# Shift rows laid down first and added by the gather, router products in column tiles, last turns between dense tiles

## The chip, the cores and the metric

The kernel runs on one core of a Trainium2 chip. The metric is the device time of one execution in microseconds (us), the median of three runs. Times inside the kernel come from one profiled execution. PE is TensorE, DVE is VectorE, ACT is ScalarE, POOL is GpSimd; SP only issues transfers. 2.4 GHz and 1.2 GHz are the two levels of TensorE's clock, shown as granted clock 1.00 and 0.50.

## The reference

One layer of a diffusion backbone with 128 context tokens and 512 latent tokens of width 2048: attention and gMLP side by side, an output projection, then a mixture of 16 experts in which each expert chooses its tokens. Everything is fp32. What the change touches:

```python
h2 = rms(x, p['g_ffn']) * (1 + sc2) + sh2
aff = softmax(h2 @ w_router)                   # 16 experts
gate, idx = top_k(swapaxes(aff, 1, 2), cap)    # 64 latent + 16 context rows for each expert
xg = h2[idx]
y = (silu(xg @ w_e1) * (xg @ w_e3)) @ w_e2 * gate
x = x + gate2 * scatter_add(y, idx)            # then a final rms and the outputs
```

`sc2` and `sh2` (scale and shift) are one row each for the context tokens and one for the latents.

## The kernel before, in words

Four phases follow one another, with a barrier at the end of each: front (adaLN rows and input projection), heads (attention), projects (three dense products, the last of which is the output projection) and experts. fp32 weights come in pieces of 128x2048 (1.05 MB). ScalarE makes a rounded high part of each (`w_hi`), VectorE the low part (`w_lo`), and PE multiplies three times (high with high, high with low, low with high; lines 107 to 109, the function `product`).

**Projects (`phase_projects`).** Chunks of 512 output columns, four pieces for each chunk, five row tiles (`t`, the first is context) for each piece. In the last dense product (`OUT`) the new residual rows are stored by POOL from `side` into `xn` in HBM, multiplied with the gain (`gained`, VectorE, into `M.xg`), turned by PE (`turn_xg`, four transposes of 128x128), copied by ScalarE (`xg_turned`), and multiplied with the router's weights (`route`: four products of 128 rows, 16 columns, accumulated in PSUM, output 16x128). VectorE adds the result of a chunk into `M.logitT` (`logit_added`). For the first three chunks these steps lie between the dense tiles of the third piece of the next chunk; for the last one all five turns and routes follow behind the last dense tile. POOL waits for the stores of `xn` before the barrier.

**Experts (`phase_experts`), its start.** PE turns `M.logitT` back into rows; VectorE scales them by 1/rms, adds the shift's logits, finds softmax and then the picks (eight rounds over the latents and two over the context, line 2132 on). ScalarE scales the rows `h_row` by 1/rms (`scale_rows`, three buffers for five tiles), POOL adds the shift row to each (line 1892) and stores it to `h` in HBM (line 1894). When all are stored and the picks are there, POOL gathers the first expert's 80 rows into `xg` (line 1876). SP has meanwhile begun to load weight pieces into eight slots; slot and order are fixed, piece n is issued when piece n-8 is split (line 91).

**Experts, the loop.** For expert i the body has 24 pieces (j = 0 to 23): eight for `w_e1` of the next expert, eight for `w_e3` of the next expert, eight for `w_e2` of this one. ScalarE and VectorE work three pieces ahead of PE in three buffers. Behind piece 16 PE turns the first twelve sixteenths of the rows of expert i+2 (`turn_rows`, line 2235), behind piece 20 the rest; that frees `xg`. VectorE makes the output rows `expert_y` at j = 19 and 23 (`out`, line 2082) from the products, `gate_now` and `gate2`. POOL's queue in iteration i is: gather of expert i+2; copies of the row numbers and gates of expert i (lines 1881, 1882, the semaphore `idx_s`, which `out` awaits); the scatter of expert i with addition into `xn` (line 1885); the wait until it has landed.

**Experts, the tail.** The last expert's rows are not scattered: POOL gathers the rows of `xn` that they belong to (line 1913), loads `xn` tile by tile (`f_x`, line 1907), ScalarE and VectorE normalise these and POOL stores the outputs; last come the rows of the last expert.

The tiles `c_st` (the front's stationary columns, 128x16x32) and `ident` stay in SBUF through all phases. The front already has products in column tiles (line 736): four products whose outputs are partitions 32j to 32j+31.

Of the kernel before, what the change touches and what calls it, by code (L numbers as in the profile page):

```python
# [14 lines left out]
P = 128  # L15
# [1281 lines left out]
def phase_projects(nc, M, I, W):  # L1297
# [8 lines left out]
    w_r = m.new("w_router_sb", [P, KT, EXPERTS], F32)  # L1306
# [5 lines left out]
    M.logitT = m.new("logitT", [EXPERTS, N_TOK], F32)  # L1312
# [18 lines left out]
    with ExitStack() as ctx:  # L1331
# [7 lines left out]
        gate_in, stored = M.pool_sem("proj_gate_in"), [M.pool_sem(f"proj_stored{t}") for t in range(TT)]  # L1339
        turn_out = [M.pool_sem(f"proj_turn_out{b}") for b in range(2)]  # L1340
# [26 lines left out]
        @block.sync  # L1367
        def _(sp):
            def load_w(n):
                if n >= 4:  # L1370
                    sp.wait_ge(w_split, n - 3)
                sp.dma_start(stage(n), WT[n // PER][(n % PER) // KG, n % KG]).then_inc(w_in[n % 4], 16)

            def load_x(s, g):
                if x_at(s, g) >= 2:
                    sp.wait_ge(x_l, x_at(s, g) - 1)
                if s == MLA and g == 0:
                    for b in range(2):
                        sp.wait_ge(M.o_out[b], 16 * (HEADS // 2))
                if s == OUT:  # L1380
                    for b in range(2):
                        sp.wait_ge(turn_out[b], 16 * ((TT * (g + 1) + 1 - b) // 2))
                src = XT[s].rearrange("(g j p) n -> g p j n", g=KG, j=KG)[g]
                sp.dma_start(x_raw[:, g % 2], src).then_inc(x_in[g % 2], 16)

            for g in range(KG):
                load_w(g)
                load_x(GM, g)
            for n in range(KG, N_PIECES):
                load_w(n)  # L1390
                s, r = n // PER, n % PER
                if s == MLA and r == KG:
                    sp.dma_start(w_r[:], I["w_router"][0].rearrange("(k p) n -> p k n", p=P)).then_inc(w_r_in, 16)
# [12 lines left out]

        @block.gpsimd
        def _(pool):
# [51 lines left out]
            for t in range(TT):  # L1460
                pool.wait_ge(stored[t], 16 * 2 * N_CH)
# [84 lines left out]
        def _(dve):  # L1546
# [40 lines left out]
            def logit_added(i):  # L1587
                dve.wait_ge(logit, TT * i + TT)
                if i:
                    dve.wait_ge(logit_sum, 2 * i)  # L1590
                for a, b, src in ((0, P, ps[6][0:EXPERTS, 0:P]), (P, N_TOK, ps[7][0:EXPERTS, :])):
# [72 lines left out]
        def _(pe):  # L1664
# [67 lines left out]
            for n in range(N_PIECES):  # L1732
# [3 lines left out]
                for t in range(TT):  # L1736
# [22 lines left out]
def phase_experts(nc, M, I, W, O):  # L1759
# [5 lines left out]
    h_row = [m.new(f"h_row{b}", [P, D], F32) for b in range(3)]  # L1765
    shift = m.new("shift2_rows", [P, 2, D], F32)
# [43 lines left out]
    with ExitStack() as ctx:  # L1810
# [7 lines left out]
        sum2, var, std, inv, scaled = (sem(f"r_{n}") for n in ("sum2", "var", "std", "inv", "scaled"))  # L1818
        log_tr, log_ok, top, neg, ex, ex_inv, aff_ok, aff_tr, aff_ev, picked, picks, pick_tr, pick_ok = (
            sem(f"r_{n}") for n in ("log_tr", "log_ok", "top", "neg", "ex", "ex_inv", "aff_ok", "aff_tr", "aff_ev", "picked", "picks", "pick_tr", "pick_ok"))  # L1820
        shift_in, h_ok, h_out = sem("r_shift_in"), sem("r_h_ok"), [M.pool_sem(f"r_h_out{b}") for b in range(3)]
# [10 lines left out]
        def _(sp):  # L1832
# [13 lines left out]
            for r in range(2):  # L1846
                sp.dma_start(shift[:, r, :], M.mod[r:r + 1, 3 * D:4 * D].to_broadcast((P, D))).then_inc(shift_in, 16)
            for q in range(PB):
                load(q, q, E13[0][0, q])
# [18 lines left out]
        def _(pool):  # L1868
            pool.sem_inc(y_free, 1)
            pool.sem_inc(x_tr, 3)  # L1870

            def gather(e):
                pool_wait(pool, x_tr, 3 * e + 3, passed)
                pool.tensor_copy(cur_g[:], rows[:, bass.ds(e, 1)]).then_inc(idx_g, 1)
                pool_wait(pool, idx_g, e + 1, passed)
                pool.indirect_dma_start(out=xg[:], out_offset=None, in_=M.h2,
# [18 lines left out]
            for b in range(3):  # L1895
                pool.wait_ge(h_out[b], 32 if b < 2 else 16)
# [11 lines left out]

            pool.tensor_copy(cur_s[:], rows[:, LAST:LAST + 1]).then_inc(idx_s, 1)
# [5 lines left out]
            for t in range(N_F):  # L1915
# [23 lines left out]
        def _(act):  # L1939
# [35 lines left out]
            def scale_rows(t):  # L1975
                if t >= 3:
                    act.wait_ge(h_out[t % 3], 16)
                for i in range(4):
                    act.activation(h_row[t % 3][:, bass.ts(i, NC)].rearrange("p (j n) -> p j n", j=KG), M.xg[i][t], ACT.Copy,  # L1979
# [70 lines left out]
        def _(dve):  # L2050
# [60 lines left out]
            dve.wait_ge(log_tr, 1)  # L2111
            for t in range(TT):
                dve.scalar_tensor_tensor(logits[:, t, :], pair[1][:, 0, bass.ts(t, EXPERTS)], st[:, 3, t:t + 1], M.shift_logit[:, min(t, 1), :],
# [108 lines left out]
        def _(pe):  # L2222
# [63 lines left out]
            for t in range(TT):  # L2286
                ins = pe.transpose(pair[1][:, 0, bass.ts(t, EXPERTS)], M.logitT[:, bass.ts(t, P)], M.ident[0:EXPERTS, 0:EXPERTS])
# [191 lines left out]
```

## Time and profile before

| | |
|---|---|
| median of 3 runs | 3500.28 us (3500.27 to 3500.41) |
| profiled execution | 3501.81 us, span 3500.0 us |
| PE busy | 3288.2 us (94%) |
| VectorE busy | 2108.0 us (60%) |
| ScalarE busy | 1409.6 us (40%) |
| POOL busy | 363.6 us (10%) |
| transfers | 790 MB, mean 226 GB/s |

The span is what the profile covers; 1.8 us of the execution lie around it, and the profiled execution is 1.5 us above the median. A busy PE is not PE at its peak: ends of matmuls are modelled, so their durations overlap, and I read the cost of a step from the start of one instruction to the start of the next. "Landing" is the time from a transfer's issue until all of it has arrived. "DMA share" is the mean busy share of the 16 DMA engines; it can read a little above 1.

### The profile page before, as it was taken

The numbers are of one execution on the slowest core, as the hardware profiler recorded it, in microseconds if no ns is written. First come the engines' busy times: TensorE is split into PE (matmuls) and PEld (weight loads), VectorE is DVE, ScalarE is ACT, GpSimd is POOL, SyncE is SP. The second block draws the span as 40 slices with busy tenths as digits, with TensorE's granted clock in tenths as the row PEclk, the third lists the DMA queues.
The fourth block names the chain that finished last, engine by engine and source line by source line (L and its number), as shares of the span: only waits on it lengthen the run. The fifth ranks groups of instructions, "written<-read, shape, count | busy, mean of one in ns | idle before, by whom it ended". The sixth has DMA issues, their size and how long they took to land. (4 is left out here: it accounts for less than half of the span.)

```text
span 3500.0 us, 39964 instructions
## 1 busy us (share of the span) xinstructions
PE 3288.2 (94%) x16088; PEld 2556.1 (73%) x16088; DVE 2108.0 (60%) x1830; ACT 1409.6 (40%) x1295; POOL 363.6 (10%) x429
## 2 busy tenths in 40 slices
PE   6889999999998899998999999939999999999995
PEld 4678878888886899986888888725666666666663
DVE  3336555555553677753232243257888898888886
ACT  3122212221211444442121222236777777777774
POOL 0020010010100000000011111030112111111102
PEclk9999999999999999999999999969999999999997
DMA  9465545465542111106253444168999999999996
GB/s 381 182 167 200 189 172 189 150 237 191 199 171 104 69 37 42 36 22 259 102 193 132 145 167 146 58 254 320 375 396 382 386 400 383 385 399 395 385 405 225
DMA packets 142462, 790.13 MB, mean 226 GB/s; under 512 B 18992, under 2 KB 30288, under 8 KB 61408
## 3 DMA queue, kind: packets, MB, share of 16 engines
q1 hardware_dynamic: 101680, 668.72, 49.5%
q0 software_dynamic: 40656, 119.60, 11.2%
q8 instruction: 95, 1.56, 0.2%
q14 instruction: 31, 0.25, 0.0%
HBM read 720.39 MB, written 67.86 MB: 225 GB/s over the span
## 5 line engine op out<-in xcount | busy, mean ns | idle before, releaser
L102 DVE TENSOR_TENSOR w_lo<-w_stage,w_hi 128x2048 fp32r<-128x2048 f32 x384 | 880.2, 2296 | 140.5 <-ACT w_hi L97 140.5
L97 ACT ACTIVATE w_hi<-w_stage 128x2048 fp32r<-128x2048 f32 x384 | 736.8, 1920 | 306.2 <-PE e_ps L109 306.1
L107 PE MATMUL i_ps<-w_hi,hT_hi 128*128 128x512 f32 (+1 forms) x1440 | 568.2, 395 | 26.0 <-DVE hT_lo L563 13.5
L108 PE MATMUL i_ps<-w_lo,hT_hi 128*128 128x512 f32 (+1 forms) x1440 | 558.7, 388 | 0.0
L109 PE MATMUL i_ps<-w_hi,hT_lo 128*128 128x512 f32 (+1 forms) x1440 | 558.5, 388 | 0.0
L107 PE MATMUL e_ps<-w_hi,xgT_hi 128*80 128x512 f32 x1024 | 404.0, 395 | 2.5 <-DVE xgT_lo L2052 2.3
L108 PE MATMUL e_ps<-w_lo,xgT_hi 128*80 128x512 f32 x1024 | 403.8, 394 | 0.0
L109 PE MATMUL e_ps<-w_hi,xgT_lo 128*80 128x512 f32 x1024 | 401.2, 392 | 0.0
L107 PE MATMUL p_ps<-w_hi,xT_hi 128*128 128x512 f32 x960 | 379.3, 395 | 15.5 <-DVE xT_lo L1547 15.5
L109 PE MATMUL p_ps<-w_hi,xT_lo 128*128 128x512 f32 x960 | 375.4, 391 | 0.0
L108 PE MATMUL p_ps<-w_lo,xT_hi 128*128 128x512 f32 x960 | 375.3, 391 | 0.0
L568 DVE TENSOR_TENSOR w_lo<-w_raw,w_hi 128x2048 fp32r<-128x2048 f32 (+1 forms) x72 | 161.8, 2247 | 348.7 <-ACT w_hi L439 348.7
L1547 DVE TENSOR_TENSOR w_lo<-w_stage,w_hi 128x2048 fp32r<-128x2048 f32 x48 | 110.0, 2292 | 392.5 <-ACT w_hi L1471 392.5
L439 ACT ACTIVATE w_hi<-w_raw 128x2048 fp32r<-128x2048 f32 (+1 forms) x72 | 135.3, 1879 | 515.1 <-PE i_ps L109 504.6
L107 PEld LDWEIGHTS i_ps<-w_hi,hT_hi 128*128 128x128 f32 x1440 | 273.0, 190 | 87.5 <-issue 26.2
L109 PEld LDWEIGHTS i_ps<-w_hi,hT_lo 128*128 128x128 f32 x1440 | 272.8, 189 | 54.9
L108 PEld LDWEIGHTS i_ps<-w_lo,hT_hi 128*128 128x128 f32 x1440 | 273.4, 190 | 52.5
L580 DVE SCALAR_TENSOR_TENSOR w_stage<-w_stage,csil 128x2048 f32<-128x2048 f32 x120 | 276.4, 2346 | 0.0
L1471 ACT ACTIVATE w_hi<-w_stage 128x2048 fp32r<-128x2048 f32 x48 | 91.9, 1915 | 442.5 <-PE p_ps L109 436.6
L107 PEld LDWEIGHTS p_ps<-w_hi,xT_hi 128*128 128x128 f32 x960 | 181.1, 189 | 52.7 <-issue 16.5
L107 PEld LDWEIGHTS e_ps<-w_hi,xgT_hi 128*80 128x80 f32 x1024 | 152.2, 149 | 86.9 <-issue 2.3
L109 PEld LDWEIGHTS e_ps<-w_hi,xgT_lo 128*80 128x80 f32 x1024 | 152.3, 149 | 84.1 <-issue 1.1
(322 smaller groups left out, 4443.7 us busy)
## 6 DMA issues: line engine op xcount, KB each, us to landing
w_stage<-in_w_e SPq DMA_DIRECT2D x384, 1024.0 KB, 9.3
w_stage<-in_w_ada SPq DMA_DIRECT2D x96, 1024.0 KB, 6.1
w_raw<-in_w_in SPq DMA_DIRECT2D x64, 1024.0 KB, 4.9
w_stage<-in_w_o_gm SPq DMA_DIRECT2D x16, 1024.0 KB, 7.8
w_stage<-in_w_o_mla SPq DMA_DIRECT2D x16, 1024.0 KB, 5.4
w_stage<-in_w_out SPq DMA_DIRECT2D x16, 1024.0 KB, 4.8
acts<-evacuated POOLq DMA_DIRECT2D x60, 256.0 KB, 3.9
side<-acts POOLq DMA_DIRECT2D x40, 256.0 KB, 5.7
```

The costliest lines, as they stand in the source:

```text
L97: act.activation(dst, src, ACT.Copy).then_inc(st.hi, 1)
L102: dve.tensor_tensor(dst, src, hi.bitcast(F32), ALU.subtract).then_inc(st.split, 1)
L107: pe.matmul(out, x_hi, w_hi, start=first, stop=False)
L108: pe.matmul(out, x_hi, w_lo, start=False, stop=False)
L109: return pe.matmul(out, x_lo, w_hi, start=False, stop=last)
L439: act.activation(w_piece(W.hi, n), draw[n % 2][:, 0:KG * WIDTH[n // KG]], ACT.Copy).then_inc(d_hi, 1)
L568: dve.tensor_tensor(w_piece(W.lo, n), draw[n % 2][:, 0:w], w_piece(W.hi, n).bitcast(F32), ALU.subtract).then_inc(d_split, 1)
L580: ins = dve.scalar_tensor_tensor(acc[r], W.stage[:, n % 2, :], csil[:, r, t:t + 1], acc[r], ALU.mult, ALU.add)
L1471: act.activation(W.hi[:, n % 2, :], stage(n), ACT.Copy).then_inc(w_h, 1)
L1547: sub = lambda out, src, hi: dve.tensor_tensor(out, src, hi.bitcast(F32), ALU.subtract)
```

## The change

1. **The shift.** POOL no longer adds the shift to `h_row`; the rows stored to `h` are without it, and SP's two loads of the shift rows are gone. A new step on POOL, `fill`, writes the shift row into all 80 places of `xg` (two transfers with a broadcast source, 64 and 16 rows), and the gather adds to them. The gather waits for its fill (semaphore `filled`). `fill(e)` waits until PE has turned the rows of expert e-1; in the loop it stands between the gather of expert i+2 and the copies and scatter of expert i. `h_row` has five buffers instead of three, so ScalarE's scaling waits for no store.
2. **The router.** Its weights lie in `c_st`, 32 columns for each 128 rows (16 of them used). The four products of `route` go to four column tiles, each a product of its own, instead of being accumulated; `logitT` has 128 partitions, its turn back is five full transposes, and VectorE adds the four groups with two reductions before the scaling.
3. **The last turns.** The turns of the last chunk's first two row tiles, and the route of the first, come between the dense tiles of the last piece (the third turn and second route right behind the last tile).
4. **Waits for the stores of `xn`** move from the end of projects into experts: SP waits ahead of its eighth load, POOL behind its stores to `h`.
5. **Tail.** `load_x(0)` stands ahead of the copies and the gather of the last rows.

```diff
-    w_r = m.new("w_router_sb", [P, KT, EXPERTS], F32)
+    w_r = M.c_st
-    M.logitT = m.new("logitT", [EXPERTS, N_TOK], F32)
+    M.logitT = m.new("logitT", [P, N_TOK], F32)
...
-            for t in range(TT):
-                pool.wait_ge(stored[t], 16 * 2 * N_CH)
...
-                out = ps[7][0:EXPERTS, bass.ts(t - 1, P)] if t else ps[6][0:EXPERTS, 0:P]
+                out = ps[7][:, bass.ts(t - 1, P)] if t else ps[6][:, 0:P]
                 for j in range(KG):
-                    ins = pe.matmul(out, w_r[:, KG * i + j, :], x[:, j, :], start=(j == 0), stop=(j == KG - 1))
+                    ins = pe.matmul(out[32 * j:32 * j + 32, :], w_r[:, KG * i + j, :], x[:, j, :], start=True, stop=True, skip_group_check=True)
...
+                    if n == N_PIECES - 1 and t >= 2:
+                        turn_xg(N_CH - 1, t - 2)
+                        if t >= 3:
+                            route(N_CH - 1, t - 3)
...
-            for t in range(TT):
+            for t in (3, 4):
                 turn_xg(N_CH - 1, t)
-                if t:
-                    route(N_CH - 1, t - 1)
+                route(N_CH - 1, t - 1)
...
-    h_row = [m.new(f"h_row{b}", [P, D], F32) for b in range(3)]
-    shift = m.new("shift2_rows", [P, 2, D], F32)
+    h_row = [m.new(f"h_row{t}", [P, D], F32) for t in range(TT)]
...
+            def fill(e):
+                pool_wait(pool, x_tr, 3 * e + 3, passed)
+                for a, b, r in ((0, CAP_LAT, 1), (CAP_LAT, SLOTS, 0)):
+                    pool.dma_start(xg[a:b, :], M.mod[r:r + 1, 3 * D:4 * D].to_broadcast((b - a, D))).then_inc(filled, 16)
             def gather(e):
-                pool_wait(pool, x_tr, 3 * e + 3, passed)
                 pool.tensor_copy(cur_g[:], rows[:, bass.ds(e, 1)]).then_inc(idx_g, 1)
                 pool_wait(pool, idx_g, e + 1, passed)
-                pool.indirect_dma_start(out=xg[:], out_offset=None, in_=M.h2,
+                pool_wait(pool, filled, 32 * e + 32, passed)
+                pool.indirect_dma_start(out=xg[:], out_offset=None, in_=M.h2, compute_op=ALU.add,
...
-            pool.wait_ge(shift_in, 32)
             for t in range(TT):
                 pool.wait_ge(scaled, 4 * t + 4)
-                pool.tensor_tensor(h_row[t % 3][:], h_row[t % 3][:], shift[:, min(t, 1), :], ALU.add).then_inc(h_ok, 1)
-                pool.wait_ge(h_ok, t + 1)
-                pool.dma_start(M.h2[bass.ts(t, P), :], h_row[t % 3][:]).then_inc(h_out[t % 3], 16)
+                pool.dma_start(M.h2[bass.ts(t, P), :], h_row[t][:]).then_inc(h_out, 16)
...
+            fill(0)
             pool.wait_ge(pick_ok, 2)
             gather(0)
+            fill(1)
             gather(1)
-            with pool.Fori(0, EXPERTS - 2) as i:
+            fill(2)
+            with pool.Fori(0, EXPERTS - 3) as i:
                 gather(i + 2)
+                fill(i + 3)
                 scatter(i)
+            gather(EXPERTS - 1)
+            scatter(EXPERTS - 3)
             scatter(LAST - 1)
...
+            load_x(0)
             pool.tensor_copy(cur_s[:], rows[:, LAST:LAST + 1]).then_inc(idx_s, 1)
...
-            for t in range(N_F):
+            for t in range(1, N_F):
                 load_x(t)
...
-                if t >= 3:
-                    act.wait_ge(h_out[t % 3], 16)
...
+            by_group = lambda ap, n: ap[:, 0:n * P].rearrange("p (t j e) -> p t e j", t=n, j=KG)[:, :, 0:EXPERTS, :]
+            dve.tensor_reduce(logits[:, 0:4, :], by_group(pair[1][:, 0, :], 4), AX.X, ALU.add).then_inc(log_sum, 1)
+            dve.tensor_reduce(logits[:, 4:5, :], by_group(pair[1][:, 1, :], 1), AX.X, ALU.add).then_inc(log_sum, 1)
+            dve.wait_ge(log_sum, 2)
```

## Rows read from the trace of the kernel before

**Rows 1.** Stretches: length; busy PE, PEld, DVE, ACT, POOL; PEclk, DMA share, GB/s.
```profile
2298.00:2353.00 55.00, 3.08 (x16) 1.61 (x17) 35.15 (x82) 22.42 (x36) 26.58 (x12) 0.51 0.94 367
...
2570.00:2638.00 68.00, 68.00 (x314) 44.41 (x313) 60.19 (x32) 48.85 (x30) 10.20 (x5) 1.00 1.01 390
```

**Rows 2.** Chain of waits ahead of the first expert: start us, us, what.
```profile
2334.74 7.71 DMA h<-h_row
...
2343.72 8.89 DMA xg<-h,rows_gather
```

**Rows 3.** Timeline of ScalarE and VectorE there: start us, us, engine, line, operation.
```profile
2310.03 0.70 ACT L1979 ACTIVATE h_row<-xg_last,r_stats 128x512 f32<-128x512 f32 x1
...
2329.72 0.17 DVE L2143 CAST rows<-e_ps 80x16 uint32<-80x16 f32 x1 [0.43 <-PE e_ps L2296]
```

**Rows 4.** Timeline of PE, one route and turn between dense tiles.
```profile
2257.06 1.05 PE L1722 MATMUL p_ps<-more,w_router_sb 128*16 128x128 f32 x8
2258.03 0.66 PE L1710 MATMUL p_ps<-ident,xg_third 128*128 128x128 f32 x4
2258.45 0.48 PE L107 MATMUL p_ps<-w_hi,xT_hi 128*128 128x512 f32 x1
```

**Rows 5.** Timeline of PE in the front: products in column tiles, then a transpose.
```profile
102.79 1.07 PE L736 MATMUL i_ps<-w_stage,c_st 128*32 128x256 f32 x16
103.80 0.44 PE L745 MATMUL i_ps<-ident,mod_rows 128*128 128x128 f32 x2
```

**Rows 6.** Ends of the phases projects and front: timelines, and DRAIN (ns, start us).
```profile
2288.24 0.54 POOL L1442 DMA_DIRECT2D xn<-side  x1 [2.18 <-DVE side L1610]
...
2294.27 0.87 DVE L1593 TENSOR_TENSOR logitT<-logitT,p_ps 16x128 f32<-16x128 f32 x2 [5.52 <-PE p_ps L1722]
...
L1331 POOLq DRAIN  x1: 5850/5850/5850, 2292.6 to 2292.6; - x1
...
1123.12 0.54 POOL L336 DMA_DIRECT2D acts<-evacuated  x1 [2.18 <-ACT evacuated L457]
...
L223 POOLq DRAIN  x1: 6295/6295/6295, 1126.5 to 1126.5; - x1
```

**Rows 7.** DMA view of 2570 to 2638, 40 slices of 1.7 us.
```profile
GB/s 429 424 429 434 414 366 251 246 328 424 424 424 419 419 414 424 424 424 424 424 419 424 419 429 414 419 424 424 414 395 434 414 299 395 366 275 275 251 328 410
DMA packets 3653, 26.51 MB, mean 390 GB/s; under 512 B 417, under 2 KB 417, under 8 KB 417
```

**Rows 8.** DMA view, issues at 2773.7, 2977.4, 2821.7: count, KB, median us to landing.
```profile
w_stage<-in_w_e SPq DMA_DIRECT2D x1, 1024.0 KB, 13.2
...
w_stage<-in_w_e SPq DMA_DIRECT2D x1, 1024.0 KB, 11.8
...
w_stage<-in_w_e SPq DMA_DIRECT2D x2, 1024.0 KB, 7.2
```

**Rows 9.** ScalarE's waits from 2436 to 3381 (us, times, longest), and one instruction.
```profile
ACT w_hi L97 <- PE e_ps L109: 266.1, 335, 1.4
...
2608.14 1.92 ACT L97 ACTIVATE w_hi<-w_stage 128x2048 fp32r<-128x2048 f32 x1 [0.86 <-PE e_ps L109]
```

**Rows 10.** Timeline of VectorE, PE and POOL in one iteration.
```profile
2609.53 1.27 DVE L2082 SCALAR_TENSOR_TENSOR expert_y<-e_ps,gate_now,gate 80x1024 f32<-80x1024 f32 x1
2610.72 2.27 DVE L102 TENSOR_TENSOR w_lo<-w_stage,w_hi 128x2048 fp32r<-128x2048 f32 x1
...
2607.94 0.44 PE L2235 MATMUL e_ps<-ident,xg 80*128 80x80 f32 x4
...
2573.23 2.68 POOL L1876 DMA_INDIRECT xg<-h,rows_gather  x1 [0.81 <-POOL rows_gather L1874]
```

**Rows 11.** Timeline of POOL and ScalarE in the tail.
```profile
3428.46 0.18 POOL L1909 COPY rows_scatter<-rows 80x1 uint32<-80x1 uint32 x1 [9.63 <-DMA xn<-expert_y,rows_scatter]
...
3432.03 3.30 POOL L1907 DMA_DIRECT2D f_x<-xn  x6
...
3442.95 1.03 ACT L2013 ACTIVATE e_ps<-f_x 128x1024 f32<-128x1024 f32 x1 [5.75 <-DMA f_x<-xn]
```

More of the change, by code:

```diff
@@ L1339, in phase_projects @@
         gate_in, stored = M.pool_sem("proj_gate_in"), [M.pool_sem(f"proj_stored{t}") for t in range(TT)]
+        M.xn_stored = stored
         turn_out = [M.pool_sem(f"proj_turn_out{b}") for b in range(2)]
@@ L1392, in _ @@
                 if s == MLA and r == KG:
-                    sp.dma_start(w_r[:], I["w_router"][0].rearrange("(k p) n -> p k n", p=P)).then_inc(w_r_in, 16)
+                    sp.dma_start(w_r[:, :, 0:EXPERTS], I["w_router"][0].rearrange("(k p) n -> p k n", p=P)).then_inc(w_r_in, 16)
                     for h in range(2):
@@ L1590, in logit_added @@
                     dve.wait_ge(logit_sum, 2 * i)
-                for a, b, src in ((0, P, ps[6][0:EXPERTS, 0:P]), (P, N_TOK, ps[7][0:EXPERTS, :])):
+                for a, b, src in ((0, P, ps[6][:, 0:P]), (P, N_TOK, ps[7][:])):
                     if i:
@@ L1817, in phase_experts @@
             sem(f"e_{n}") for n in ("x_tr", "x_hi", "x_lo", "sil_ok", "hid_ok", "h_tr", "h_hi", "h_lo", "y_ev"))
-        sum2, var, std, inv, scaled = (sem(f"r_{n}") for n in ("sum2", "var", "std", "inv", "scaled"))
+        sum2, var, std, inv, scaled, log_sum = (sem(f"r_{n}") for n in ("sum2", "var", "std", "inv", "scaled", "log_sum"))
         log_tr, log_ok, top, neg, ex, ex_inv, aff_ok, aff_tr, aff_ev, picked, picks, pick_tr, pick_ok = (
             sem(f"r_{n}") for n in ("log_tr", "log_ok", "top", "neg", "ex", "ex_inv", "aff_ok", "aff_tr", "aff_ev", "picked", "picks", "pick_tr", "pick_ok"))
-        shift_in, h_ok, h_out = sem("r_shift_in"), sem("r_h_ok"), [M.pool_sem(f"r_h_out{b}") for b in range(3)]
+        filled = M.pool_sem("rows_filled")
+        h_out = M.pool_sem("r_h_out")
         f_in, f_out, g_in = [M.pool_sem(f"f_in{b}") for b in range(N_F)], [M.pool_sem(f"f_out{b}") for b in range(N_F)], sem("f_g_in")
@@ L1844, in last @@
                         load(n + 4 * c + q, (j0 + 4 * c + q) % NS, E2[e, c, q])
-            for r in range(2):
-                sp.dma_start(shift[:, r, :], M.mod[r:r + 1, 3 * D:4 * D].to_broadcast((P, D))).then_inc(shift_in, 16)
             for q in range(PB):
+                if q == PB - 1:
+                    for t in range(TT):
+                        sp.wait_ge(M.xn_stored[t], 16 * 2 * (D // NC))
                 load(q, q, E13[0][0, q])
@@ L1887, in scatter @@
                 pool_wait(pool, scattered, 16 * e + 16, y_free)
-            pool.wait_ge(shift_in, 32)
             for t in range(TT):
                 pool.wait_ge(scaled, 4 * t + 4)
-                pool.tensor_tensor(h_row[t % 3][:], h_row[t % 3][:], shift[:, min(t, 1), :], ALU.add).then_inc(h_ok, 1)
-                pool.wait_ge(h_ok, t + 1)
-                pool.dma_start(M.h2[bass.ts(t, P), :], h_row[t % 3][:]).then_inc(h_out[t % 3], 16)
-            for b in range(3):
-                pool.wait_ge(h_out[b], 32 if b < 2 else 16)
+                pool.dma_start(M.h2[bass.ts(t, P), :], h_row[t][:]).then_inc(h_out, 16)
+            for t in range(TT):
+                pool.wait_ge(M.xn_stored[t], 16 * 2 * (D // NC))
+            pool.wait_ge(h_out, 16 * TT)
+            fill(0)
             pool.wait_ge(pick_ok, 2)
             gather(0)
+            fill(1)
             gather(1)
-            with pool.Fori(0, EXPERTS - 2) as i:
+            fill(2)
+            with pool.Fori(0, EXPERTS - 3) as i:
                 gather(i + 2)
+                fill(i + 3)
                 scatter(i)
+            gather(EXPERTS - 1)
+            scatter(EXPERTS - 3)
             scatter(LAST - 1)
@@ L1975, in scale_rows @@
             def scale_rows(t):
-                if t >= 3:
-                    act.wait_ge(h_out[t % 3], 16)
                 for i in range(4):
-                    act.activation(h_row[t % 3][:, bass.ts(i, NC)].rearrange("p (j n) -> p j n", j=KG), M.xg[i][t], ACT.Copy,
+                    act.activation(h_row[t][:, bass.ts(i, NC)].rearrange("p (j n) -> p j n", j=KG), M.xg[i][t], ACT.Copy,
                                    scale=st[:, 3, t:t + 1]).then_inc(scaled, 1)
@@ L2286, in _ @@
             for t in range(TT):
-                ins = pe.transpose(pair[1][:, 0, bass.ts(t, EXPERTS)], M.logitT[:, bass.ts(t, P)], M.ident[0:EXPERTS, 0:EXPERTS])
+                ins = pe.transpose(pair[1][:, t // 4, bass.ts(t % 4, P)], M.logitT[:, bass.ts(t, P)], M.ident[:])
             ins.then_inc(log_tr, 1)
```

2 lines of the change are left out of this document (1 added, 1 removed).

## The prediction

> **What bounds the kernel now.** I read the table of stretches first. In the expert loop one iteration has PE busy for all of its time, at a granted clock of 1.00 (the 2.4 GHz level), and the DMA share is 1.01 at 390 GB/s; in the 55 us ahead of the first expert PE works 3.1 us [rows 1]. So the loop goes at PE's pace with DMA just keeping up, and the stage ahead of it is a chain in which PE has no part. The chain of waits names that chain: the store of the row tile scaled last, issued at 2334.74, lands after 7.71 us, and the first gather, issued at 2343.72, takes 8.89 us [rows 2]. The picks are ready long before, at 2329.9 [rows 3]. Last I read the loop's transfers: how fast they go and how late they land [rows 7, 8].
>
> **Part 1, projections: router products in column tiles.** A step of four products now holds PE from 2257.06 to 2258.03, 0.97 us; the four turns behind it last until 2258.45, 0.42 us [rows 4]. There are 15 such steps between dense tiles, all with PE busy without a gap. The trace has tiled products with 32 columns: eight of 128x256, two rounds of four, take 1.01 us from their start to the next instruction, 0.50 a round [rows 5]. The new step is one round of half that width: 0.25 us if time goes by width, 0.50 if it doesn't; since each product brings its weights as there, I take 0.50. Saved: 15 x 0.47 = 7.0 us. Two turns (2 x 0.42) and one route (0.50) now lie ahead of the last dense tile: +1.3. Dense work ends 5.7 us sooner (15 x 0.72 - 1.1 = 9.7 at 0.25; 1.8 us later if tiles don't overlap, since three steps are put in all the same).
> The Trainium skill, TensorEngine Tiling (Array Packing), section Tiling Modes, says that a change of tiling mode drains TensorE. By that rule each step pays twice for switching. The trace agrees as far as it goes: a full-width instruction follows the tiled step there [rows 5], and what leaving the mode costs is in its 1.01 us; a drain as dear as the step itself would take the gain away, which is rival C's time.
>
> What follows the last dense tile is not PE. POOL's DRAIN at the phase's end starts at 2292.6 and lasts 5.85 us, to 2298.45, while VectorE, whose last sums wait for the last route, is done by 2295.2 [rows 6]; the next phase starts behind the DRAIN. It ends 10.2 us after POOL's last store was issued (2288.24); in the front phase the DRAIN ends 9.7 us after the last full-height store (1123.12 to 1132.8) though it started only 3.4 us later [rows 6]. So I take it that the end hangs on the last store, which moves with the dense work: gain 5.7 us, and the earlier last turns and the dropped waits for the stores give nothing. If the drain instead lasts 5.85 us from wherever it starts, it begins some 3.5 us sooner relative to that store, and 3.5 us more are won. On the other side of the barrier VectorE adds two reductions and a wait (some 0.6 us by its small instructions) and PE five full transposes; ScalarE is busy with the first scaled rows meanwhile, so I cost them at nothing; the bound is +0.6.
>
> **Part 2, from scaled rows to the first gather.** Removed: five additions on POOL, the two broadcasts of the shift (2.1 MB), and the wait for one of three buffers. Times from the stage's start (2298.6 now). ScalarE has the third scaled tile at 11.4 (2310.7) [rows 3] and needs 2.4 us a tile: the last at 17. Picks at 31. Now DMA decides. Eight weight pieces (8.4 MB), the stores (5.2 MB) and gate2 (0.66 MB) must share 420 GB/s: 14.3 MB, 34 us. Stores and weights are in flight together to the end, so the stores land at about 33.5. Then come, in a row, the fill (0.66 MB beside one new weight piece, about 5.5 us), POOL's 0.8 us, and the gather: 8.9 now, 10 with its addition. That is 50, where now it lands at 54.0 (2352.6). Gain 3.5 us after a little loss; from 1 (the fill as slow as the loaded gather's 8.9) to 8 (stores landed by 29).
>
> **Part 3, the loop: bytes.** Each expert gets one more transfer, 80 rows of 8 KB = 0.66 MB, and its gather adds. An iteration moves 26.5 MB at 390 GB/s, 67.9 us. Outside two dips it runs flat at 419 to 429 GB/s [rows 7]. PE asks for 24 pieces of 1.05 MB in that time, 371 GB/s. So the gathers' and scatters' cost is paid out of the rest. The dips: the gather's slices (366, 251, 246, 328) lack 0.86 MB against 424, 2.0 us; the scatter-add's (299, 395, 366, 275, 275, 251, 328) lack 1.32 MB, 3.1 us. The difference, 1.1 us, is my price for adding in a gather; the bounds are 0 and twice that. The fill costs 0.66 MB / 424 = 1.55 us.
> How much is free? The time to landing of a weight piece says it: just after the gather 13.2 us in the iteration from 2770, 11.8 three iterations later, 7.2 before the scatter [rows 8]. From the high it fell by 0.47 us per iteration, so about 0.5 us of DMA time per iteration is spare. Excess: 1.55 + 1.1 - 0.5 = 2.1 us per iteration (1.0 to 3.2).
> The excess first lengthens the landing. A piece is issued when the piece eight before it is split and wanted when PE has finished the third before it: 8 x 2.76 less the 4.4 us of ScalarE (1.92) and VectorE (2.27) [rows 9, 10], 17.7 us, and 1.1 us of slack behind it: 18.8. No wait of ScalarE on a transfer shows in the loop now, all 335 are on PE [rows 9]. Twelve iterations have both fill and adding gather, one before them only the latter: from 12.5, between the two peaks read, 12.5 + 1.1 + 12 x 2.1 = 38.8, less 18.8: **20 us** that PE must wait, with 6 and 33 us at the two ends.
> The Trainium skill, Trainium Kernel Development and Optimization, section Key Constraints, says that transfers issued from SP, ACT and POOL run on the same 16 DMA engines and interleave. By that, a fill on POOL's queue takes its time from the weights, which the sum assumes; if POOL had bandwidth of its own, the term would be 0.
>
> **Part 4, the loop: order on POOL.** The fill waits for the last turns of the rows before (PE, 2607.94 to about 2608.5), and rows_scatter and gate_now, which VectorE's output product awaits, are now queued behind it. With 0.3 us to react, two issues of 0.54 [rows 6] and 0.3 us for the two copies (one takes 0.18) [rows 11] they come at 2610.3; the product starts at 2609.53 now, so it is 0.8 us late. Behind it stands the split of the piece that PE wants at 2613.7 (24 more products of 0.23 after the turns); it ends at 2613.0 now [rows 10]. 0.1 us per iteration is lost, 1.4 in all, and that only if DMA is not the bound: the same stall isn't paid twice. I take 0 beside the 20. The first two experts' fills have over 40 us until they are needed.
>
> **Part 5, the tail.** The first f_x load no longer stands behind two copies and the indirect gather of the last rows: now its issue starts at 3432.03 [rows 11], 3.5 us after the scatter has landed and the first copy has begun (3428.46), then at that point. ScalarE waits for that load until 3442.95 and everything behind it follows: -3.5 us (0 to 4.5).
>
> **Sum.** Profiled execution 3501.81: - 5.7 - 3.5 - 3.5 + 20 = 3509.1. That execution is 1.5 above the median, so 3507.6.
>
> **Rivals.** A, the backlog absorbs it: if adding costs nothing, the fill's source row makes no dip and two to three times the spare time exists (the landing stops falling near 6 us before each scatter, so some may be hidden), excess stays under 0.5 us and 12.5 + 6 does not reach 18.8. Time 3500.3 - 12.7 = 3487.6, or 3484 with the shorter drain. For it: no transfer holds anything now. Against it: share 1.01 and the flat 424. It decides at 0.5 us of excess. B, POOL's issue is slow beside VectorE: the gather's issue takes 2.68 us there [rows 10]. If the first fill is issued at that price the output product is 2.9 late, 2.2 after slack, 13 times: 3487.6 + 28 = 3516. Against it: direct DMAs beside VectorE take 0.54. C, column tiles do not overlap at this width: 7.5 us lost again, 3515. Against it: rows 5.
>
> **Chances.** Forecast 0.40, spread over 3498 to 3518; A 0.38; B 0.10; C 0.12. A measurement of this kernel can tell 0.2% (7 us) from no change. Faster: 0.34 of A. Within: 0.04 of A, 0.18 of the forecast, 0.04 of C: 0.26. Slower: 0.22 of the forecast, B, 0.08 of C: 0.40. The range for 8 in 10 reaches from A's lower value to the forecast with 3 us of excess: 3484 to 3523. The forecast alone: 3498 to 3518.
>
> **What would show it.** Landing times that climb by 2 us per iteration to 18 and then waits of ScalarE on transfers, with an iteration of 70 us: part 3 right. Landing that stays near 13 with 67.9 us: A. VectorE waiting ahead of the output product for more than 1 us: B. A route step above 0.6 us: part 1 wrong. A DRAIN that ends less than 9 us after the last store: 3.5 us more. Stores that land after 36: part 2 too large. Wrong altogether if the picks, not the stores, end last.

## The result and the profile after

| | before | after |
|---|---|---|
| median, beside each other on one chip | 3500.35 us | 3521.01 us |
| profiled execution | 3501.81 us, span 3500.0 | 3519.99 us, span 3518.2 |
| from the stage's start to the first gather's landing | 54.0 us | 55.1 us |
| loop, first to last scatter issued | 926.6 us | 953.3 us |

The changed kernel is slower: ratio 1.0057 (95% interval 1.0044 to 1.0071), 20.7 us. The prediction said 3507.6, so 7.3 us slower: the direction and the place of the loss, the loop's transfers, were right, the size was not. All three terms of the loop's excess were off, and the largest error was nearly cancelled by the two others.

I read the stretches first, as in [rows 1] (length; busy PE, PEld, DVE, ACT, POOL; PEclk, DMA share, GB/s):

```profile
2287.00:2342.00 55.00, 3.37 (x13) 1.60 (x13) 30.76 (x84) 22.16 (x36) 5.51 (x9) 0.50 0.97 341
2560.00:2628.00 68.00, 67.91 (x313) 44.02 (x312) 59.93 (x32) 48.78 (x29) 10.27 (x7) 1.00 1.02 383
3050.00:3120.00 70.00, 68.50 (x313) 43.92 (x312) 60.08 (x32) 48.38 (x29) 8.29 (x8) 1.00 1.02 386
```

Early in the loop PE still fills its 68 us; later the same work (313 products) takes 70 us or more. The clock is unchanged at 1.00, and the DMA rate has not risen although there is more to move. The waits of 2420 to 3400 (us, times, longest) say who is late:

```profile
ACT w_hi L97 <- PE e_ps L109: 222.5, 268, 2.6
...
ACT w_hi L97 <- DMA w_stage<-in_w_e: 74.4, 63, 3.3
...
PE e_ps L107 <- DVE w_lo L102: 16.7, 16, 2.5
...
DVE expert_y L2094 <- POOL gate_now L1891: 10.9, 13, 0.8
```

Against [rows 9] the second line is new: ScalarE waits 63 times for a weight piece. The last line is the product behind POOL's fill, 0.8 us late in each of 13 iterations. The issues of the same stretch (count, KB, median us to landing):

```profile
w_stage<-in_w_e SPq DMA_DIRECT2D x338, 1024.0 KB, 15.6
xg<-mod POOLq DMA_DIRECT2D x13, 512.0 KB, 9.3
xg<-mod POOLq DMA_DIRECT2D x13, 128.0 KB, 10.0
...
xg<-h,rows_gather POOLq DMA_INDIRECT x13, 10.6
```

A weight piece takes 15.6 us to land (9.4 from 2436 to 3381 of before); by iteration its median climbs from 10.6 us to 16.4 in two iterations and stays there. The DMA view of one iteration (40 slices of 1.7 us, then POOL's queue: packets, MB, share of the 16 engines), to be read against [rows 7]:

```profile
GB/s 439 414 443 419 434 323 255 275 371 410 429 410 429 414 434 414 429 419 424 424 414 434 414 434 410 429 318 251 241 202 376 419 424 419 424 414 419 347 265 275
...
q0 software_dynamic: 301, 1.97, 13.1%
```

The gather's dip (323, 255, 275, 371) is what it was, although it now adds. The fill has a dip of its own (318, 251, 241, 202, 376): five slices lack 732 GB/s against 424, 1.24 MB, 2.9 us, on top of its own bytes.

Ahead of the loop, the chain of waits (start us, us) as in [rows 2], and the two rows at the end of the projects phase as in [rows 6]:

```profile
2304.23 17.16 DMA h<-h_row
...
2322.70 11.46 DMA xg<-mod
...
2335.07 7.03 DMA xg<-h,rows_gather
```

```profile
2279.57 0.54 POOL L1443 DMA_DIRECT2D xn<-side  x1 [3.20 <-ACT more L1499]
...
L1331 POOLq DRAIN  x1: 5850/5850/5850, 2280.9 to 2280.9; - x1
```

In steps, by the two profiled executions: the expert stage starts 11.7 us sooner (ScalarE's first instruction 2286.97, was 2298.64); its front part takes 1.1 us more; until the first scatter is issued (2478.99, was 2487.30) 2.2 us more go, and the lead is 8.3; the loop loses 26.7; the tail gains 2.8 up to the last stores' issue, and the stretch behind that issue is 2.7 longer. Sum +18.2, the difference of the spans.

### The profile page after: what moved, and what is told of

The parts are those of the page before. It is cut to its first block and busy times, and to the rows that moved or that the text cites. A ratio compares the mean times of both kernels' runs of the same rounds, so it can differ in the third digit from the quotient of the medians.

```text
span 3518.2 us, 40008 instructions
## 1 busy us (share of the span) xinstructions
PE 3284.8 (93%) x16088; PEld 2539.8 (72%) x16088; DVE 2104.2 (60%) x1832; ACT 1408.4 (40%) x1295; POOL 338.4 (10%) x456
## 5 line engine op out<-in xcount | busy, mean ns | idle before, releaser
L107 PE MATMUL i_ps<-w_hi,hT_hi 128*128 128x512 f32 (+1 forms) x1440 | 568.0, 394 | 25.7 <-DVE hT_lo L563 12.9
L107 PE MATMUL e_ps<-w_hi,hiddenT_hi 128*80 128x512 f32 x512 | 205.1, 401 | 10.0 <-DVE w_lo L102 7.6
## 6 DMA issues: line engine op xcount, KB each, us to landing
w_stage<-in_w_e SPq DMA_DIRECT2D x384, 1024.0 KB, 15.4
```

Source lines behind the costliest of these rows:

```text
L107: pe.matmul(out, x_hi, w_hi, start=first, stop=False)
```

## The experiments

The profiled executions of the kernels that have the change's projections phase differ by some 4 us in where the expert stage starts (2286.7 to 2290.9), so I compare stretches inside a run: "loop" is the time from the first to the last scatter's issue; before has 926.6.

| kernel | median us | ratio to before (95%) | loop us | what the fill writes |
|---|---|---|---|---|
| no_shift | 3482.97 | 0.9933 to 0.9966 | 926.6 | nothing |
| fill_no_add | 3519.23 | 1.0031 to 1.0064 | 953.3 | 64 + 16 rows of 8 KB |
| fill_rows | 3525.10 | 1.0048 to 1.0082 | 959.9 | the same, from 80 source rows |
| fill_act | 3519.84 | 1.0043 to 1.0077 | 957.8 | the same, issued by ScalarE |
| fill_sp | 3509.79 | 1.0012 to 1.0041 | 963.3 | the same, issued by SP |
| fill_split | 3527.71 | 1.0058 to 1.0092 | 956.1 | 64 + 16 rows of 4 KB, twice |
| fill_128 | 3548.04 | 1.0113 to 1.0147 | 980.7 | 64 + 64 rows of 8 KB |
| fill_even | 3486.34 | 0.9938 to 0.9969 | 926.7 | 128 rows of 5 KB, one transfer |
| fill_one_128 | 3494.83 | 0.9972 to 0.9990 | 929.7 | 128 rows of 8 KB, one transfer |
| all_but_fill | 3489.95 | 0.9953 to 0.9978 | 926.7 | nothing, POOL adds |
| adds_five | 3491.53 | 0.9951 to 0.9978 | 926.7 | nothing, POOL and VectorE add |
| weights_held | 3486.82 | 0.9944 to 0.9972 | 926.7 | nothing, as adds_five |

**Is it the fill, the addition, or POOL's order?** Theory 1 holds the fills' transfers to be the loss, rival 2 the addition, rival 3 the copies that stand behind the fill.

no_shift and fill_no_add:

```diff
-                for a, b, r in ((0, CAP_LAT, 1), (CAP_LAT, SLOTS, 0)):       # no_shift alone
-                    pool.dma_start(xg[a:b, :], M.mod[r:r + 1, 3 * D:4 * D].to_broadcast(...)).then_inc(filled, 16)
-                pool.indirect_dma_start(out=xg[:], ..., in_=M.h2, compute_op=ALU.add,     # both
+                pool.indirect_dma_start(out=xg[:], ..., in_=M.h2,
```

> The changed kernel without the fill and with a plain gather (the shift is left out of the rows of the experts). Everything else of the change stays. Theory 1 (the fills' transfers are the whole loss of the loop): iteration back at 67.9 us, landings near 13 us, 26.6 us of loop won back; the first gather starts at stage start + 35 instead of + 48, so 12 us more; 3521.0 - 26.6 - 12 = 3482. Theory 2 (the addition is the loss) and theory 3 (the order on POOL is) expect the same here: this run sets the floor. If the loop still takes 70 us per iteration, something else of the change costs it, and all three fall.

> The changed kernel with its fills, but the gather overwrites instead of adding (so the shift is left out of the rows). Theory 1 (fill): 3521, within 2 us; the slices of the gather in the DMA view stay as they are (some 0.8 MB short), the fill's stay (1.2 MB short). Theory 2 (the addition costs 1 us or more per gather): at least 13 us less, 3508 or lower. Theory 3 (order on POOL): 3521.

Without the fill the loop is back to 926.6 us and the median at 3483.0, 38.0 below the changed kernel: 26.7 of the loop, 7.9 in the stage's front part (first gather landed 47.2 us after the stage's start, not 55.1), 1.7 from there to the first scatter and 2.7 behind the last scatter, less 0.6 by which the profiled execution starts the stage later. Without the addition nothing changes: the loop has the same 953.3 us. Theory 1 stands and rival 2 falls: a gather that adds costs the loop no time.

**What makes the fill so dear?** Its bytes are 1.55 us, its whole cost 4.4. First its source and its queue:

```diff
-                    pool.dma_start(xg[a:b, :], M.mod[r:r + 1, 3 * D:4 * D].to_broadcast((b - a, D)))
+                    pool.dma_start(xg[a:b, :], M.shift_80[a:b, :])          # fill_rows: written once before
+                    act.dma_start(xg[a:b, :], M.mod[r:r + 1, ...])          # fill_act: behind rows_hi(i + 2, 2)
+                    sp.dma_start(xg[a:b, :], M.mod[r:r + 1, ...])           # fill_sp: behind an iteration's ninth piece
```

> The changed kernel, but the fill reads 80 different rows of HBM (copies of the shift rows, written once at the start of the experts) instead of one row 64 times and another 16 times. Same bytes, same queue, same place in POOL's order. Theory 1a (reading one row over and over makes the dip): the 2.9 us dip per fill goes, 1.55 us for the bytes stay, 0.5 are spare: 1.05 us of excess per iteration, some 14 us over the loop less 7 that the landings take up: 7 us lost instead of 26.6, and the first fill takes 5.5 us instead of 11.5: 3497. Theory 1b (the dip comes with any fill on POOL's queue): 3521. Theory 3 (order on POOL): 3521.

> The changed kernel, but ScalarE issues the fills (behind its copies of the last turned rows) instead of POOL; the source is still one row read 64 and 16 times. Theory 1a (the one source row makes the dip): 3521 within 3 us, dip of 1.2 MB still there. Theory 1b (the dip belongs to POOL's queue): as 1.55 us per fill alone, about 3500. Theory 3 (the copies that VectorE waits for stand behind the fill on POOL): these 0.8 us per iteration go, 3510, and the landings stay late.

> The changed kernel, but SP issues the fills, in its own queue behind the ninth weight piece of an iteration; nothing of the fill is left on POOL. Theory 4a (a second queue beside SP's makes the dip, for the engines switch between queues): the fill costs its bytes alone, 1.55 us, of which 0.5 are spare; loop lost 14 us less the 7 that the landings take up; 3503. Theory 4b (the dip comes with what is written, 8 KB into each of 80 partitions, whoever issues it): the dip of some 1 MB stays and the time with it, 3518 to 3521. Theory 3 (order on POOL): 3510.

The rates of 2560 to 2630 in 40 slices of 1.75 us, fill_rows first, then fill_act, then fill_sp:

```profile
GB/s 272 384 440 431 417 435 356 248 262 328 417 417 435 417 421 421 412 431 421 412 440 412 421 426 412 435 421 253 229 229 169 421 431 403 435 426 304 295 295 412
```

```profile
GB/s 435 426 421 360 276 257 375 407 431 426 407 426 431 407 435 412 426 426 412 431 426 407 435 407 272 262 192 407 421 431 407 431 421 412 360 272 267 435 421 421
```

```profile
GB/s 440 403 440 356 243 281 375 393 445 421 407 440 421 412 431 393 449 426 398 440 417 417 435 403 435 426 407 435 426 403 295 215 225 360 323 295 286 375 445 421
```

The dip is in each: 253, 229, 229, 169 (1.43 MB short) with 80 source rows, 272, 262, 192 (0.96 MB) from ScalarE's queue, 295, 215, 225, 360 (1.05 MB) from SP's own. So neither the one source row nor the queue makes it, and theories 1a, 1b and 4a fall. Rival 3 falls with fill_act: nothing of the fill is left on POOL there, VectorE's output product waits for no copy any more, and the time is the changed kernel's (3519.8). The 0.8 us per iteration are real, but hidden. fill_sp's median, 3509.8, is what neither theory forecast (3503, or 3518 to 3521). Its executions lie far apart (3501.7 to 3530.4) and the profiled one is among its slowest; why that order scatters so I leave open, and I use of it only that the dip is there.

Then how the fill is laid out. fill_even leaves the shift out of the rows (its gather is plain), the other three compute everything:

```diff
+                pool.dma_start(h_row[0][:, 0:SLOTS * D // P], M.mod[1:2, 3 * D:3 * D + SLOTS * D // P].to_broadcast((P, SLOTS * D // P)))   # fill_even
...
+                    for h in range(2):                                                       # fill_split
+                        pool.dma_start(xg[a:b, bass.ts(h, D // 2)], M.mod[r:r + 1, bass.ds(3 * D + h * D // 2, D // 2)].to_broadcast(...))
...
+                for a, b, r in ((0, CAP_LAT, 1), (CAP_LAT, P, 0)):                           # fill_128
+                    pool.dma_start(xg_all[a:b, :], M.mod[r:r + 1, 3 * D:4 * D].to_broadcast((b - a, D)))
...
+                pool.dma_start(xg_all[:], M.shift_128)                                       # fill_one_128
```

> The changed kernel with a plain gather (the shift is left out of the rows) whose fill writes the same 0.66 MB, from POOL's queue, as 128 rows of 5 KB into 128 partitions instead of 80 rows of 8 KB into 80; the gather then overwrites it. Theory 4b in its form of partitions (80 of 128 partitions load the engines or their ways into SBUF unevenly): the dip of 1.2 MB (2.9 us) goes, the fill costs 1.55 us, 3503 or so. Theory 4a (two queues): the dip stays, 3519.

> The changed kernel; each fill goes in two halves of the columns, 160 rows of 4 KB instead of 80 of 8 KB, into the same 80 partitions, from POOL's queue. Theory 4b (the dip comes from filling 80 of 128 partitions): it stays, 3519 to 3521, iteration some 70 us. Theory 4c (the dip comes from long rows, few and large packets; the even fill had 5 KB): the dip goes, landings stay near 10 us, 67.85 us an iteration, 3487 to 3490.

> The changed kernel; the fill writes 8 KB rows into all 128 partitions (the 48 below the 80 that count get a shift row that nobody reads): 1.05 MB instead of 0.66. Theory 4b (80 of 128 partitions): no dip; 2.5 us of bytes, of which the even fill's 1.55 were hidden without a trace, so 0 to 0.9 us of excess per iteration, of which the landings take up the first 8: 3487 to 3495. Theory 4c (long rows): the dip is as large as before or larger, and the bytes are more: 3521 or above.

> The changed kernel; each fill is one transfer of 128 rows of 8 KB (1.05 MB) from 128 rows of HBM that were written with the shift rows during the projects phase; the 48 rows that nobody needs fall into the unused partitions under the 80. What sets the dip is still open: fills of 64 and 16 rows dip whoever issues them, with one or many source rows, with rows of 4 or 8 KB, also as twice 64 rows over all partitions; one transfer of 128 rows of 5 KB does not. Theory 4e (a transfer costs its bytes alone only when it spans the 128 partitions by itself, as the weight pieces and the even fill do): no dip, landings near 10 to 14 us, 67.9 to 68.5 us an iteration, 3487 to 3495. Theory 4f (the even fill was cheap for its 5 KB rows, or for its fewer bytes, or since it read the front of one row): the dip is there as in the fill of 128 rows in two halves, 3540 or above.

The same view, fill_even (its fill is issued at 2597.2, slice 22), fill_split (2603.6, slice 25), fill_128 (2605.4, slice 26) and fill_one_128 (2597.6, slice 22):

```profile
GB/s 426 426 421 257 253 318 431 412 426 421 421 426 417 417 431 417 421 421 426 417 426 421 421 421 414 424 421 421 421 426 417 421 421 421 276 267 356 431 421 440
```

```profile
GB/s 262 351 440 431 412 435 370 253 267 328 426 407 426 426 412 426 426 421 426 417 431 417 412 426 431 412 426 297 286 274 290 300 426 398 435 417 421 426 328 281
```

```profile
GB/s 290 276 365 412 440 426 417 365 281 272 323 407 435 417 417 435 412 421 426 407 435 421 412 435 417 421 431 407 300 239 248 229 229 375 431 417 417 276 262 365
```

```profile
GB/s 426 426 426 290 276 253 398 426 421 421 431 407 421 435 407 431 431 407 431 417 417 435 407 426 431 412 426 426 417 426 417 417 440 403 281 295 323 431 440 421
```

fill_even runs through its fill at 414 to 426 GB/s; the two dips that are left are the gather's and the scatter's. It is faster than its theory forecast (3486.3, not 3503), since more DMA time is spare than the 0.5 us assumed (below). Halving the rows' length (fill_split: 297, 286, 274, 290, 300) does nothing, and 128 partitions filled by two transfers of 64 (fill_128: 300, 239, 248, 229, 229, 375) are worse than 80: theory 4b in its first form and 4c both fall. One transfer of the same 1.05 MB over the same 128 partitions has no dip at all, and takes 53 us off the time (3548.0 to 3494.8). That is theory 4e: **in these runs a transfer costs its bytes alone when it spans all 128 partitions by itself**, and more when it spans 64, whatever lies beside it. These two differ also in their source (two rows repeated, or 128 rows); but fill_rows dips with 80 source rows, and fill_even doesn't with one row repeated. They differ in the number of transfers too. That isn't the reason either: fill_split doubles the number over the same partitions (four instead of two), and its loop is only 2.8 us longer than the changed kernel's, where fill_128's is 51 us longer than fill_one_128's. And the gather is one transfer of 80 rows with a dip of its own.

The Trainium skill, SBUF — State Buffer, sections "Door 1: The DMA port swizzle" and "Can I just issue two DMAs to hit both halves?", states this rule: partitions 0 to 63 reach 8 of SBUF's 16 ports, and only one transfer over all 128 partitions reaches all 16. The trace agrees: 202 to 251 GB/s at the bottom of the fill's dip against 424. From its figures (27.2 GB/s a port; 0.52 MB over 8 ports, 0.13 MB over 4) the fill would take an estimated 3.6 us, where the dip and the bytes measure 4.4. I had not weighed this rule in the prediction.

**Everything but the fill, and more room ahead of the loop.**

```diff
 # all_but_fill: the kernel before + tiles, last turns, stored waits, load_x(0) first
 # adds_five: also
+    h_row = [m.new(f"h_row{t}", [P, D], F32) for t in range(TT)]
+    shift = Map(nc, W.lo_at).new("shift2_rows", [P, 2, D], F32)
+                if s0 == 16:                                     # between two rounds of the picks
+                    dve.scalar_tensor_tensor(h_row[TT - 1] ..., M.xg[i][TT - 1], st[:, 3, TT - 1:TT], shift ..., ALU.mult, ALU.add)
 # weights_held: also
+            for q in range(4, PB):
+                if q == 5:
+                    sp.wait_ge(h_out, 16 * TT)
+                load(q, q, E13[0][0, q])
```

> The kernel before with everything of the change but the fill and the adding gather: router products in column tiles, last turns between dense tiles, waits for the stores moved, first tail load sooner; POOL adds the shift as before, with three buffers. By theory 1 (parts add up, the drain lasts 5.85 us from wherever it starts): the expert stage starts 11.7 us sooner, its front part takes 54.0 us as before, the loop 67.9 us an iteration, the tail 2.8 us less (as in the kernel without a shift): 3500.4 - 14.5 = 3486. Rival: the stage's front part gets longer than 54.0 us, since transfers are its bound and they start sooner relative to the last stores of the projects phase: 3489 or more; or the tail keeps its 86.06 us: 3489.

> As the kernel before with everything but the fill, and POOL's additions spread: five buffers for the scaled rows (no wait of ScalarE for stores), the shift rows in the room of the weights' low parts, and VectorE scales and adds the last tile between two rounds of the picks. Theory (the last store sets the first gather): four additions of 5.1 us from stage start + 7.9 put the last store's issue at + 29 instead of + 36; 16.4 MB at 424 GB/s must have moved, + 39, so the stores have landed by + 39 to + 40 instead of + 43.8, the picks come 2.6 us later (+ 33.6) and don't matter; the gather lands at + 49 instead of + 54: 5 us under the kernel with everything but the fill, 3481. Rival: the picks or the additions beside VectorE get so much slower that nothing is won: 3486.

> As adds_five (everything but the fill, additions spread over POOL and VectorE), and SP holds back three of the eight first weight pieces until the rows' stores have landed. Theory (transfers are the bound of the stage's front part: 400 GB/s and more from its start to the last store's landing): 3.1 MB less ahead of the stores, 7.5 us, so they land at + 36 instead of + 43.8 and the first gather at + 46: 7 us under adds_five, 3484. Rival: the pieces held back, or those behind them, now come late and PE waits for them when it starts: 3491.

all_but_fill is faster than both kernels, 12.0 us under before (14.5 were forecast; 2.1 of the difference is a later start of the stage than the changed kernel's). Its ratio to before, 0.9965, is also below the 0.9981 of fill_one_128 (the intervals just overlap), so even the fill without a dip shows no gain over leaving the fill out. Its stage starts at 2289.00 (9.6 sooner), the first gather lands 53.5 us later (54.0 before), the loop is 926.7, and from the last scatter's issue to the end it takes 83.4 us (86.1). adds_five gains nothing on it. Its chain and that of weights_held:

```profile
2322.35 11.89 DMA h<-h_row
...
2335.82 8.59 DMA xg<-h,rows_gather
```

```profile
2323.30 5.05 DMA h<-h_row
...
2333.59 10.20 DMA xg<-h,rows_gather
```

In adds_five the last store is issued 31.5 us after the stage's start instead of 36.0 and lands where it did, at 43.4 (43.5): transfers bound this stretch, not POOL. Holding three weight pieces back confirms it (landed after 38.7 us), but in the profiled execution the row copy ahead of the gather took 3.85 us on POOL, and the gather 10.2, so that it landed after 54.2 us:

```profile
2328.82 3.85 POOL L1883 COPY rows_gather<-rows 80x1 uint32<-80x1 uint32 x1 [4.95 <-DMA h<-h_row]
```

That copy runs beside VectorE's low parts. The profiled execution was the slowest of its five (3484.5 to 3491.9), so what the holding is worth, up to 5 us, stays open; its interval overlaps that of all_but_fill.

## Why the prediction had direction and place right and its terms wrong

The forecast was 7.3 us slower and the measurement 20.7, nearly three times that. 3521.0 lies inside the range for 8 in 10 (3484 to 3523), which was wide because it covers rival A as well; it lies 3 us above the forecast's own 3498 to 3518. By the profiles the forecast erred by 6.0 us too little gain in part 1, 4.6 too much in part 2, 6.7 too little loss in part 3 and 3.4 too much gain in part 5; another 2.2 us, between the first gather and the first scatter, it did not have. That the parts' errors partly cancel is luck.

**Part 1** (forecast 5.7 gained, profile 9.6 to 11.7). The step of column tiles was forecast at 0.50 us and is 0.35, from 2257.36 to 2257.71:

```profile
2257.36 0.43 PE L1721 MATMUL p_ps<-more,c_st 128*32 128x128 f32 x8
2257.71 0.66 PE L1709 MATMUL p_ps<-ident,xg_third 128*128 128x128 f32 x4
2258.13 0.47 PE L107 MATMUL p_ps<-w_hi,xT_hi 128*128 128x512 f32 x1
```

So 15 steps save 9.3 us instead of 7.0; rival C is out, and whatever switching the mode costs is inside 0.35. POOL's last store is issued 8.7 us sooner (2279.57, was 2288.24). The second step that failed is "the end hangs on the last store". POOL's DRAIN lasts 5.85 us in [rows 6] and in every kernel here, wherever it starts. It started 4.4 us after the last store's issue while POOL waited for the stores, and starts 1.3 us after it now that the waits have gone: with the 8.7 us this is the 11.7 by which the stage starts sooner. The alternative that the text held ready (some 3.5 us more) was the right one; I had chosen against it on the phase of the front, where the DRAIN lasts another time.

**Part 2** (forecast 3.5 gained, 1.1 lost). Stores landed at 34.4 us after the stage's start for 33.5 forecast, and the picks came at 29: the byte sum was good. What failed is the fill at 5.5 us; it took 11.5. Here the layout is not the main reason: fill_even's and fill_one_128's first fills, without a dip later on, still take 10.1 and 10.7 us. The likely reason is the weight pieces that are in flight at this point: a plain gather issued there takes 10.1 us (no_shift), and 6.0 where it comes a fill later (fill_no_add). No run separates it. The gather behind it took 7.0 instead of 10, which gave a part back. The 2.2 us between this landing and the first scatter have no cause that a run separates.

**Part 3** (forecast 20, measured 26.7). The mechanism was right: landings climb, then ScalarE waits. The sum per iteration was 1.55 + 1.1 - 0.5 = 2.1. The terms measure otherwise. The addition: 0, not 1.1. The fill: 1.55 + 2.9 = 4.4, not 1.55; this is the step that failed most. And the spare time: in fill_one_128 the fill costs its bytes alone, 1.05 MB / 424 = 2.5 us, and the median landing of a weight piece climbs from 10.8 us (iteration from 2493) to 15.2 (from 2901):

```profile
w_stage<-in_w_e SPq DMA_DIRECT2D x24, 1024.0 KB, 10.8
...
w_stage<-in_w_e SPq DMA_DIRECT2D x24, 1024.0 KB, 15.2
```

That is 4.4 us in six iterations, 0.7 each: 1.8 us of the 2.5 are spare. fill_even fits: 1.55 us of bytes, and its landings fall from 10.5 to 8.8. So the excess is 4.4 - 1.8 = 2.6 us; late in the loop an iteration takes 70.4 (3387.61 less 2894.53, seven of them), 2.6 above 67.85. That the excess was forecast at 2.1 and measured 2.6 is again luck: 2.9 us too little for the dip stand against 1.1 too much for the addition and 1.3 too little spare time. The spare time was misread from single landings of before, which fell by 0.47 an iteration [rows 8]. The medians by iteration do not fall: in eight of them from 2493 to 3377 they lie between 8.7 and 10.3 us. They have reached a floor, and a landing there says nothing of how much more would fit. The dip of the fill was costed at nothing since the DMA view of before has no fill. The nearest rows it had were the gather's dip, 2.0 us for the same 80 rows into the same tile [rows 7]; taken over, they would have put the fill at 3.6 us.

**Part 4** (forecast 0 behind 0.8 us each): right on both counts, 10.9 us of waits in 13 iterations, and fill_act shows that they cost nothing while DMA is the bound.

**Part 5** (forecast 3.5 gained). ScalarE waits 2.7 us for its first tile instead of 5.8 [rows 11], and the last stores are issued 70.6 us after the last scatter, 73.4 before: 2.8 gained. What follows the issue gave it back: 15.4 us to the end, 12.7 before. The code there is the same. The issue in after, before (span 3500.0), fill_act (3516.4) and fill_split (3526.1):

```profile
3502.84 0.95 POOL L1944 DMA_INDIRECT out_y_sample<-xg,rows_lat  x1 [6.49 <-DVE xg L2235]
```

```profile
3487.33 0.94 POOL L1930 DMA_INDIRECT out_y_sample<-xg,rows_lat  x1 [6.50 <-DVE xg L2219]
```

```profile
3503.68 0.94 POOL L1943 DMA_INDIRECT out_y_sample<-xg,rows_lat  x1 [6.49 <-DVE xg L2243]
```

```profile
3508.08 0.94 POOL L1945 DMA_INDIRECT out_y_sample<-xg,rows_lat  x1 [6.49 <-DVE xg L2236]
```

All 14 profiles fall into an order by what the fills put on POOL's queue. Without any (before, no_shift, fill_act, fill_sp and the three of the last group) the stretch is 12.7 to 12.9 us, with one transfer for each of the 16 fills (fill_even, fill_one_128) 14.0 to 14.1, with two (after, fill_no_add, fill_rows, fill_128) 15.3 to 15.5, with four (fill_split) 18.0. So each transfer of the fills on POOL's queue adds 1.3 us in 16, some 0.08 us each, behind the last store, wherever it stood in the program. What does this is not shown; the forecast had no such term.

**The rivals.** B (a slow issue on POOL) is out: the fill's two issues take 1.12 us together (from 2601.00) and the output product is 0.8 us late, not 2.9. A (nothing is lost in the loop) needed an excess under 0.5 us; with one fill over all partitions it is 0.7. Two of its three conditions did hold, an addition for nothing and three times the spare time and more, and the third, no dip from the fill, decided against it.

## What to carry to other kernels

Where DMA is near its bound, cost a transfer by what it does to the rate of the others, not by its bytes: a fill of 64 and 16 partitions cost 4.4 us here where 1.55 us of bytes would have been hidden, and padding it to one transfer over 128 partitions, with 60% more bytes, gave 23.6 of the loop's 26.7 us back. The time to landing tells of a backlog, not of spare time once it has reached its floor; only an added load measures that. And work that leaves an idle engine for a full one (here POOL's additions, replaced by transfers) has to be paid for on the full one.

## What the runs showed of the hardware that I had not expected

- A gather with addition costs the loop no more than a plain one: 953.3 us either way. Alone, behind the first fill, it took 7.0 us against 6.0.
- The same 1.05 MB as two transfers of 64 partitions or as one of 128: 980.7 against 929.7 us of loop, late in it 72.6 against 68.6 us an iteration.
- POOL's DRAIN at the end of projects lasts 5850 ns from its own start, wherever that is (2280.6 to 2292.6 in 14 profiles).
- The stretch from the last stores' issue to the end is 12.7 to 12.9, 14.0, 15.4 or 18.0 us with 0, 16, 32 or 64 transfers of fills on POOL's queue.
- A column-tiled step of four products of 128 columns takes 0.35 us from start to start, between full-width instructions.
- A copy of 80 numbers on POOL takes 0.18 us alone [rows 11], but 2.2 us in the tail of after and 3.85 us in weights_held, beside VectorE. The Trainium skill, SBUF — State Buffer, section "Who interferes with whom", says that a VectorE instruction with both inputs in SBUF keeps POOL from reading there; these copies agree with it. The one of 2.2 us runs from 3447.40 to 3449.62, beside VectorE's low part from 3447.28 to 3449.57, and the one of 3.85 us ends at 2332.67, beside low parts that end at 2332.62.
